# All 16 weight tiles of the second layer's scale modulation as VectorE multiply-adds, landing in two places beside the load ring

## The chip, the cores and the metric

The kernel runs on one core of a Trainium2 chip. The metric is the device time of one execution in microseconds (us); the time before is the median of three runs.

## The reference

Two layers of an adaLN-modulated mixer block over 256 latent and 256 context tokens, D = 2048, all in float32. Cut to what matters here:

```
def modulate(x, norm_g, ada):
    shift, scale, gate = jnp.split(ada, 3, axis=-1)
    return rmsnorm(x, norm_g) * (1 + scale) + shift, gate
...
def mixer_layer(x, xc, c_act, cc_act, norm_g, w_ada, b_ada, w_in, ...):
    h, gate = modulate(x, norm_g, (c_act @ w_ada + b_ada)[:, None, :])
    hc, gate_c = modulate(xc, norm_g, cc_act @ w_ada + b_ada)
    u = h @ w_in
    uc = hc @ (w_in[:, :OFF_MEM_END] if last else w_in)
    ...
    x = x + gate * (jnp.concatenate([y_conv, y_lru, y_attn], axis=-1) @ w_out)
    if not last:
        xc = xc + gate_c * (jnp.concatenate([yc_conv, yc_lru, yc_attn], axis=-1) @ w_out)
```

The change concerns the `scale` third of `c_act @ w_ada + b_ada` and of `cc_act @ w_ada + b_ada` in the second layer: two vectors of 2048, each times a 2048 x 2048 matrix. The weights of layer 1 don't depend on layer 0, so this product can be made while layer 0 is still being computed.

## The kernel before

**Blocks.** Each layer works through 56 blocks of weights of 1 MB (`NB = 56`): blocks 0 to 39 are the input projection (0 to 3 LRU, 4 to 7 keys and values, 8 to 15 convolution, 16 to 31 queries and attention gates, 32 to 39 the other gates), blocks 40 to 55 (`B_OUT = 40`) the output projection, one for each 128 of the output's channels. A block is 16 k-tiles. Float32 products are made of three passes: ScalarE copies a half of the block's weights to a rounded form (`hi`, L1050), VectorE subtracts it from the weights (`lo`, L1410), and TensorE runs high by high, low by high and high by low (L826, L827, L828): 48 matmuls of 512 columns for a block of layer 0.

**The order of work** is written out by hand. Each engine runs its own list, and all of them wait on semaphores. While TensorE is at block b, ScalarE makes `hi` and VectorE `lo` of block b+2, and VectorE brings block b's result out of PSUM (L1596 and L1605 for gate blocks, L1614 for output blocks). SyncE issues the loads in the order of `stream()` into a ring of three slots of 1 MB (`NRAW = 3`, `raw`); a load waits until the tile that had its slot before has been read, and everything behind it in the queue waits too. Behind w(b) for output blocks comes `residual` (L539), which brings 256 KB of the input back for the addition.

**Modulation of layer 1** is made during layer 0 and needs `w_ada` of layer 1, which is 48 tiles of 1 MB (16 each for shift, scale and gate).
- Shift runs on TensorE between blocks: `ada_mm` (L656), four matmuls of 512 columns for a tile, which lie side by side in the array.
- Gate runs on VectorE: `gate_acc(k)` multiplies tile k, one row of the matrix to a partition, by its value of c and adds it to a sum in `kv` (L1441 for tile 0, L1444 for the others). `gate_sum` (L675) adds up over partitions on TensorE at the start of layer 1. In the last two blocks the gate tiles lie ahead of the sums of squares for layer 1's norm (L1467, L1520, L1578 on VectorE, L1091 on ScalarE), which L731 and L733 add up on TensorE.
- Scale is split. Tiles 0 to 7 run on TensorE like shift, two at the end of each of blocks 24, 26, 28 and 30. Tiles 8 to 15 run on VectorE, `scale_acc(k)`: two instructions for a tile, one for c and one for the context's vector, into `qreg` (L1453 for the first tile, L1456 for the others). `scale_sum` (L666, at block `SCALE_SUM = NB - 4`, that is 52) adds the partitions up and onto what TensorE had.

A scale tile of a block up to `SCALE_RING = 39` is loaded into the ring; later ones land in `glu`, which is free by then. `SCALE_ON_DVE` says at which block which tile is added, `gate1_plan()` the same for gate.

**bd** holds the LRU's block-diagonal gate matrices. In layer 0 it also holds keys' parts for attention, until the last group's P·V product (`pv`, L920 to L922, at block 38). GpSimd then clears it for layer 1 (L632), and four small loads (`gate_weights`, L530) bring layer 1's matrices, issued behind the load of block 44. They are first read in layer 1 at 869.7 us (L858).

The functions that the diff touches, and what calls them:

Of the kernel before, what the change touches and what calls it, by code (L numbers as in the profile page):

```python
# [26 lines left out]
DT = D // P  # L27
# [13 lines left out]
SHIFT, SCL, GATE = range(3)  # L41
# [11 lines left out]
NB = len(BLOCKS[0])  # L53
# [31 lines left out]
PW_AT = 35  # L85
LAST_GROUPS = [22, 25, 29, 32]
GATE1_AT = 39
SCALE_ON_DVE = {36: [8], 37: [9], 40: [10], 42: [11], 44: [12], 46: [13], 48: [14], 50: [15]}
SCALE_RING = 39
SCALE_SUM = NB - 4  # L90
TP_LAG = [1, 2]
# [45 lines left out]

def gate1_plan():

    return {B_OUT - 2: [0], B_OUT + 1: [1, 2], **{B_OUT - 1 + k: [k] for k in range(3, DT)}}  # L140

# [108 lines left out]
def program(nc, io, known):  # L252
    ctx = ExitStack()
    with ctx:
# [88 lines left out]
        SLOT, n, ringed = [], 0, 0  # L343
        for i, item in enumerate(STREAM):
            if item[0] == "scale" and item[1] in beside_ring:
                SLOT.append(GLU_SLOT)
            elif i >= opened:
                SLOT.append(ringed % NRAW)
                ringed += 1
            elif item[0] == "chunk":  # L350
                SLOT.append(CHUNK_SLOTS[item[1] % 2])
            else:
                SLOT.append(ADA0_SLOTS[n % len(ADA0_SLOTS)])
                n += 1
# [161 lines left out]
        @block.sync  # L516
        def _(sp):
            sp.dma_start(small[:, 0:N_FIRST], io["small"][:, 0:N_FIRST]).then_inc(*C.up("small_in", by=16))
            for g in range(DT // XPART):
                sp.dma_start(Y[:, XPART * g:XPART * (g + 1), :], io["xT"][:, XPART * g:XPART * (g + 1), :]  # L520
                             ).then_inc(*C.up(f"x_in{g}", by=16))
            sp.dma_start(T[:, 5, 0:3 * P], io["exact"]).then_inc(*C.up("exact_in", by=16))

            def gate_weights(l):

                sp.wait_ge(*(C.at("bd_zero", l) if l not in ROW_GATES else used(last_of(BD_SLOT))))
                for g in range(2):
                    for j in range(2):
                        side, part = (64 * (g ^ j), 0) if l in ROW_GATES else (64 * j, g)
                        sp.dma_start(bd[64 * j:64 * j + 64, part, :, side:side + 64],  # L530
                                     io["lru_w"][l, g, j]).then_inc(*C.up("bd_in", l, g, j, by=16))

            def residual(m):

                if m < 2:
                    sp.wait_ge(*C.at("att_out", 0, max(groups(0))))
                else:
                    sp.wait_ge(*C.at("evac_dve", B_OUT + m - 2))
                sp.dma_start(T[:, m % 2, :], io["xT"][:, m, :]).then_inc(*C.up(f"xs{m % 2}", m, by=16))  # L539

            def turn(l, s):

                b = ROPE_AT[l][s]
                kind, i = BLOCKS[l][b]
                order = list(ROPE_AT[l].values())
                n = order.index(b)
                sp.wait_ge(*C.at("evac_act", l * NB + b))
                if n >= 2:
                    sp.wait_ge(*C.at("rope", l, *BLOCKS[l][order[n - 2]]))
                elif l:  # L550
                    sp.wait_ge(*C.at("ln_n", 0, CT - 1))
                    sp.wait_ge(*C.at("ada_tp", 1, GATE))
                if l == 0:
                    for step, items in PLAN.items():
                        for rows in items:
                            if step < s and rows[2] == DT - 1:
                                sp.wait_ge(*C.at("ada_tp", *rows[:2]))
                for quad in range(0, P, 32):
                    sp.dma_start(turned_of(l, b)[quad:quad + 32, :], rope_of(l, b)[quad ^ 32:(quad ^ 32) + 32, :]
                                 ).then_inc(*C.up(f"turned{n % 2}", l, kind, i, quad, by=16))  # L560

            def turns(item):

                l, s = divmod(item[1] - 1, NB) if item and item[0] == "w" else (0, 0)
                return (l, s) if s in ROPE_AT[l] else None

            for i, item in enumerate(STREAM):
                freed = None
                if SLOT[i] in SLOT[:i]:
                    freed = i - 1 - SLOT[:i][::-1].index(SLOT[i])  # L570
                    sp.wait_ge(*used(freed))
                head = turns(STREAM[freed]) if freed is not None else None
                if head and head[0]:
                    turn(*head)
                dst = slot(i)
                if item[0] == "w":
                    src = io["w_blocks"][item[1]]
                elif item[0] == "chunk":
                    src = io["w_blocks"][0:OPEN[0], :, item[1] * CK * P:(item[1] + 1) * CK * P].rearrange("b p c -> p b c")
                    dst = dst[:, 0:OPEN[0] * CK * P].rearrange("p (b c) -> p b c", b=OPEN[0])  # L580
                elif item[0] == "open":
                    src = io["w_blocks"][NB:NB + SIDE, :, item[1] * QT * P:(item[1] + 1) * QT * P
                                         ].rearrange("b p c -> p b c")
                    dst = dst.rearrange("p (b c) -> p b c", b=SIDE)
                elif item[0] == "ada0":
                    kind, c, g = item[1:]
                    k0, n = group_k(c)
                    rows, cols, at0 = D // n, n * P, kind * D + k0 * P
                    src = io["w_ada"][0, g * rows:(g + 1) * rows, at0:at0 + cols].rearrange("(j p) c -> p j c", p=P)
                    dst = dst.rearrange("p (j c) -> p j c", c=cols)  # L590
                elif item[0] == "pw":
                    src = io["pw"][item[1]]
                elif item[0] == "gate":
                    src = io["w_ada"][1, item[1] * P:(item[1] + 1) * P, GATE * D:(GATE + 1) * D]
                elif item[0] == "scale":
                    if beside_ring and item[1] == beside_ring[0]:
                        sp.wait_ge(*C.at("evac_dve", BLOCKS[0].index(("cg", CT - 1))))
                    src = io["w_ada"][1, item[1] * P:(item[1] + 1) * P, SCL * D:(SCL + 1) * D]
                else:
                    l, kind, k = item[1:]  # L600
                    src = io["w_ada"][l, k * P:(k + 1) * P, kind * D:(kind + 1) * D]
                sp.dma_start(dst, src).then_inc(C.sem(f"raw{SLOT[i]}"), 16)  # L602
                if item == ("chunk", 1):
                    sp.dma_start(small[:, N_FIRST:N_SMALL], io["small"][:, N_FIRST:N_SMALL]
                                 ).then_inc(*C.up("later_in", by=16))
                if item == ("w", OPEN[0] + 1):
                    gate_weights(0)
                if head and not head[0]:
                    turn(*head)
                if item == ("w", B_OUT + 4):  # L610
                    gate_weights(1)
                if item[0] == "w" and 0 <= item[1] - B_OUT - 2 < DT - 2:
                    residual(item[1] - B_OUT - 2)
                elif item[0] == "open" and item[1] < 2:
                    residual(DT - 2 + item[1])
            for m, n in final_parts():
                sp.wait_ge(*C.at("final", m))
                sp.dma_start(io["out"][:, m:m + n, :], Y[:, m:m + n, 0:LAT]).then_inc(*C.up("stored", by=16))
            sp.wait_ge(*C.ago("stored"))
# [3 lines left out]
        def _(pool):  # L623
# [4 lines left out]
            nc.gpsimd.memset(pick[:, 32:33], 1.0).then_inc(*C.up("pick_set"))  # L628
            for l in range(LAYERS):
                if l:  # L630
                    pool.wait_ge(*C.at("pv", l - 1, max(groups(l - 1))))
                    nc.gpsimd.memset(bd[:, :, :, :], 0.0).then_inc(*C.up("bd_zero", l))  # L632
                else:
                    for slot_of_q in Q_SLOTS:
                        pool.wait_ge(*used(last_of(slot_of_q)))
# [9 lines left out]
        def _(pe):  # L645
# [14 lines left out]
            def scale_sum():  # L660

                pe.wait_ge(*C.at("pick_set"))
                pe.wait_ge(*C.at("scale_acc", DT - 1, 1))
                for i in range(2):
                    for j in range(4):
                        last = mm(psA[32 * j:32 * j + 32, :], pick[:, 32 - i:64 - i], scale_part(i)[:, j * TOK:(j + 1) * TOK],  # L666
                                  start=False, stop=(i == 1), tile_position=(0, 32 * j))
                last.then_inc(*C.up("ada_mm", 1, SCL, DT - 1))

            def gate_sum():  # L670
# [1293 lines left out]
```

## Time and profile before

| | |
|---|---|
| median of 3 runs | 1247.78 us (1247.63 to 1248.28) |
| the profiled execution | 1247.64 us |
| its span from first to last instruction | 1245.7 us |
| TensorE clock granted in it, mean | 0.995 of 2.4 GHz |
| busy: TensorE, VectorE, ScalarE | 1203.5, 827.3, 555.5 us |

Some 1.9 us lie outside the span. In rows of the timeline the columns are start (us), duration (us), engine, line, operation, output <- inputs, shape, and in square brackets how long the engine was idle just before and what released it. A row with "x8" stands for eight instructions in a run, with the time of all of them. Matmuls overlap by some 0.15 us at their ends, and other instructions by some 0.08, so that starts, and not durations, are to be compared. Layer 0 ends near 797 us. "+" and "-" in the diff below are lines of the kernel after and before; numbers of lines (L...) are those of the kernel before, unless said otherwise.

### The profile page before, as it was taken

How to read it: one execution, taken by the hardware profiler on the slowest of the kernel's cores; microseconds unless marked ns; L12 is line 12 of the kernel's file. 1: busy time of each engine (PE TensorE's matmuls, PEld its weight loads, DVE VectorE, ACT ScalarE, POOL GpSimd, SP SyncE). 2: the span in 40 equal slices, each digit the busy share in tenths (PEclk: the TensorE clock that was granted, in tenths of full speed). 3: DMA queues.
4: the chain of work that ended last, by engine and by line, in shares of the span. 5: the costliest groups of instructions: out<-in, count | busy, mean ns of one | idle time of the engine just before them, and what ended most of it. 6: DMA issues, size and time to landing. Idle time of an engine off the chain costs nothing.

```text
span 1245.7 us, 16857 instructions
## 1 busy us (share of the span) xinstructions
PE 1203.5 (97%) x6790; PEld 971.9 (78%) x6790; DVE 827.3 (66%) x1268; ACT 555.5 (45%) x873; POOL 10.2 (1%) x13
## 2 busy tenths in 40 slices
PE   2899999999999999999999999999999999999996
PEld 1556777667778777886888887988978988899995
DVE  5444546767666677663787877695899977647554
ACT  5222446652224433464342222354865445475542
POOL 0000100000000000000000001000000000000000
PEclk9999999999999999999999999999999999999998
DMA  9999856556753354211549776343332634325542
GB/s 334 350 349 348 251 208 240 203 207 248 270 218 127 140 187 185 75 68 68 177 158 344 259 286 229 109 145 134 138 106 77 223 133 149 132 102 199 177 170 68
DMA packets 80893, 236.34 MB, mean 190 GB/s; under 512 B 9392, under 2 KB 54192, under 8 KB 59440
## 3 DMA queue, kind: packets, MB, share of 16 engines
q1 hardware_dynamic: 80816, 235.27, 53.5%
q8 instruction: 53, 0.87, 0.3%
q14 instruction: 24, 0.20, 0.1%
HBM read 230.54 MB, written 2.10 MB: 187 GB/s over the span
## 4 chain that ended last, share of the span: by engine, by line
PE 84%; DVE 5%; SPq 4%; DMA 4%; ACT 2%; issue 1%; DVEq 0%; ACTq 0%
PE psum_block L826 21%; PE psum_block L828 21%; PE psum_block L827 21%; SPq L602 3%; PE psum_ada L656 3%; DMA raw<-in_w_ada 2%; PE psum_scores L908 1%; PE psum_scores L895 1%; DVE w_lo L1410 1%; PE psum_scores L928 1%; DVE Y L1691 1%; PE psum_ada L703 1%; DMA glu<-in_w_ada 1%; DMA bd<-in_w_ada 1%; PE psum_misc L955 1%; PE psum_scores L858 1%
## 5 line engine op out<-in xcount | busy, mean ns | idle before, releaser
L826 PE MATMUL psum_block<-h_hi,w_hi 128*128 128x256 f32 (+1 forms) x1648 | 562.4, 341 | 0.6 <-DVE h_lo L1402 0.3
L828 PE MATMUL psum_block<-h_hi,w_lo 128*128 128x256 f32 (+1 forms) x1648 | 553.3, 336 | 0.0
L827 PE MATMUL psum_block<-h_lo,w_hi 128*128 128x256 f32 (+1 forms) x1648 | 553.2, 336 | 0.0
L1410 DVE TENSOR_TENSOR w_lo<-raw,w_hi 128x1024 fp32r<-128x1024 f32 x210 | 254.7, 1223 | 287.7 <-ACT w_hi L1050 287.4
L1050 ACT ACTIVATE w_hi<-raw 128x1024 fp32r<-128x1024 f32 x210 | 220.2, 1057 | 419.5 <-PE psum_block L828 380.0
L826 PEld LDWEIGHTS psum_block<-h_hi,w_hi 128*128 128x128 f32 x1648 | 312.7, 190 | 53.4 <-issue 17.6
L827 PEld LDWEIGHTS psum_block<-h_lo,w_hi 128*128 128x128 f32 x1648 | 312.9, 190 | 33.6 <-issue 2.6
L828 PEld LDWEIGHTS psum_block<-h_hi,w_lo 128*128 128x128 f32 x1648 | 312.7, 190 | 32.4
L1691 DVE SCALAR_TENSOR_TENSOR Y<-glu,small,Y 128x512 f32<-128x512 f32 (+1 forms) x240 | 130.4, 612 | 0.0
L1217 ACT ACTIVATE T<-psum_scores,stats 128x512 f32<-128x512 f32 (+1 forms) x48 | 28.9, 615 | 46.5 <-DVE stats L1739 46.5
L1104 ACT ACTIVATE h_hi<-T,ada 128x256 fp32r<-128x256 f32 x64 | 28.5, 501 | 41.6 <-DVE T L1486 41.6
L1410 DVE TENSOR_TENSOR w_lo<-qreg,w_hi 128x1024 fp32r<-128x1024 f32 (+1 forms) x16 | 17.5, 1092 | 33.4 <-ACT w_hi L1050 32.3
L656 PE MATMUL psum_ada<-raw,cstat 128*32 128x512 f32 x320 | 38.5, 598 | 1.1 <-DVE ada L1475 1.1
L1444 DVE SCALAR_TENSOR_TENSOR kv<-raw,cstat,kv 128x2048 f32<-128x2048 f32 x15 | 35.2, 2344 | 1.1 <-DMA raw<-in_w_ada 1.0
L1223 ACT ACTIVATE T<-T,stats 128x512 f32<-128x512 f32 (+1 forms) x48 | 27.4, 640 | 13.6 <-DVE stats L1749 13.6
L1648 DVE SCALAR_TENSOR_TENSOR Y<-qreg,small,Y 128x512 f32<-128x512 f32 x48 | 32.5, 746 | 0.0
L1050 ACT ACTIVATE w_hi<-qreg 128x1024 fp32r<-128x1024 f32 (+1 forms) x16 | 15.1, 945 | 33.8 <-DMA qreg<-in_w_blocks 33.8
L1079 ACT ACTIVATE T<-Y 128x512 f32<-128x512 f32 (+1 forms) x46 | 24.4, 544 | 10.8 <-DVE Y L1614 8.6
L1492 DVE SCALAR_TENSOR_TENSOR h_lo<-T,ada,h_hi 128x256 fp32r<-128x256 f32 x64 | 27.8, 480 | 1.3 <-ACT h_hi L1104 1.3
L1486 DVE SCALAR_TENSOR_TENSOR T<-Y,A,tbuf 128x256 f32<-128x256 f32 x64 | 27.6, 481 | 0.6
L1456 DVE SCALAR_TENSOR_TENSOR qreg<-glu,cstat,qreg 128x2048 f32<-128x2048 f32 x12 | 27.6, 2345 | 0.0
L1467 DVE TENSOR_TENSOR T<-T 128x512 f32<-128x512 f32 (+1 forms) x42 | 25.1, 598 | 2.8 <-ACT T L1079 1.3
(222 smaller groups left out, 1215.0 us busy)
## 6 DMA issues: line engine op xcount, KB each, us to landing
raw<-in_w_blocks SPq DMA_DIRECT2D x105, 1024.0 KB, 4.8
raw<-in_w_ada SPq DMA_DIRECT2D x75, 1024.0 KB, 7.1
glu<-in_w_ada SPq DMA_DIRECT2D x11, 1024.0 KB, 8.1
qreg<-in_w_blocks SPq DMA_DIRECT2D x8, 896.0 KB, 11.6
kv<-in_w_ada SPq DMA_DIRECT2D x5, 1024.0 KB, 12.0
bd<-in_w_ada SPq DMA_DIRECT2D x5, 1024.0 KB, 11.9
Y<-in_xT SPq DMA_DIRECT2D x8, 512.0 KB, 8.0
T<-in_xT SPq DMA_DIRECT2D x16, 256.0 KB, 5.8
```

The source lines that it names most:

```text
L602: sp.dma_start(dst, src).then_inc(C.sem(f"raw{SLOT[i]}"), 16)
L656: last = mm(psA[32 * j:32 * j + 32, :], cstat[:, c_at(k):c_at(k) + 32], w[:, j * TOK:(j + 1) * TOK], start=(k == 0), stop=(k == DT - 1), t ...
L826: mm(ps[:, cols], hi, hh[:, k, t], start=(at == 0), stop=False)
L827: mm(ps[:, cols], hi, hl[:, k, t], start=False, stop=False)
L828: last = mm(ps[:, cols], lo, hh[:, k, t], start=False, stop=(at == DT - 1))
L1050: fn(wh[:, u % 4, 0:cols.stop - cols.start], raw_of(item)[:, cols], ACT.Copy).then_inc(*C.up("hi", u))
L1104: fn(hh[:, k, tokens(i)], T[:, k % 2, tokens(i)], ACT.Identity, bias=ada[:, l, i, SHIFT * DT + k:SHIFT * DT + k + 1]).then_inc(*C.up("h_hi ...
L1217: fn(T[:, g, k0:TOK], psS[:, g, k0:TOK], ACT.Exp, scale=SCALE, bias=st[:, 1, g:g + 1], accum_out=st[:, 2, g:g + 1]).then_inc(*C.up("att_ex ...
L1410: V.tensor_tensor(wl[:, u % 4, 0:n], raw_of(item)[:, cols], wh[:, u % 4, 0:n].bitcast(F32), ALU.subtract).then_inc(*C.up("lo", u))
L1444: stt(acc, w, cstat[:, c_at(k):c_at(k) + 1], acc, ALU.mult, ALU.add).then_inc(*C.up("gate_acc", k))
L1648: stt(out, x, lcw[:, c, k:k + 1], out, ALU.mult, ALU.add).then_inc(*C.up("taps", l, t, d))
L1691: stt(out, x, dwh[:, c:c + 1], out, ALU.mult, ALU.add).then_inc(*C.up("conv", l, t, k))
```

## The change

All 16 tiles of scale now go through `scale_acc` on VectorE, so that no `ada_mm` of scale is left on TensorE, and `scale_sum` begins the sum in PSUM itself (it therefore waits until shift has been read out of PSUM). Tiles 0 to 4 are added at blocks 36 to 38 and come through the ring. Tiles 5 to 15 are added at blocks 40 to 45 and 47 to 51, one for each block, and land by turns in `glu` and in `bd`. Since `bd` is taken until tile 14 (block 50), it is cleared behind that, and `gate_weights(1)` is issued behind the load of ("open", 0), the first quarter of layer 1's opening blocks. The gate tiles move too: two of them at block 53 and one at 54, and none doubled at block 41.

```
-SCALE_ON_DVE = {36: [8], 37: [9], 40: [10], 42: [11], 44: [12], 46: [13], 48: [14], 50: [15]}
+SCALE_ON_DVE = {36: [0, 1], 37: [2, 3], 38: [4], 40: [5], 41: [6], 42: [7], 43: [8], 44: [9], 45: [10], 47: [11], 48: [12],
+                49: [13], 50: [14], 51: [15]}
...
-    return {B_OUT - 2: [0], B_OUT + 1: [1, 2], **{B_OUT - 1 + k: [k] for k in range(3, DT)}}
+    return {B_OUT - 2: [0], B_OUT + 1: [1], **{B_OUT + k: [k] for k in range(2, DT - 3)}, NB - 3: [13, 14], NB - 2: [15]}
...
             if item[0] == "scale" and item[1] in beside_ring:
-                SLOT.append(GLU_SLOT)
+                SLOT.append((GLU_SLOT, BD_SLOT)[beside_ring.index(item[1]) % 2])
...
-                    if beside_ring and item[1] == beside_ring[0]:
+                    if item[1] == beside_ring[0]:
                         sp.wait_ge(*C.at("evac_dve", BLOCKS[0].index(("cg", CT - 1))))
+                    elif item[1] == beside_ring[1]:
+                        sp.wait_ge(*C.at("pv", 0, max(groups(0))))
...
-                if item == ("w", B_OUT + 4):
+                if item == ("open", 0):
                     gate_weights(1)
...
-                    pool.wait_ge(*C.at("pv", l - 1, max(groups(l - 1))))
+                    pool.wait_ge(*C.at("scale_acc", beside_ring[-1 - len(beside_ring) % 2], 1))
...
                 pe.wait_ge(*C.at("scale_acc", DT - 1, 1))
+                pe.wait_ge(*C.at("ada_out", 1, SHIFT))
...
-                                  start=False, stop=(i == 1), tile_position=(0, 32 * j))
+                                  start=(i == 0), stop=(i == 1), tile_position=(0, 32 * j))
```

VectorE's list at blocks 36 and 37, before; L1453 and L1456 are scale tiles (two instructions each), L1410 is `lo` of a block's half, L1729 the low part of the attention weights, which TensorE's P·V product waits for.

```order
L1453 TENSOR_SCALAR qreg<-raw,cstat 128x2048 x2
L1410 TENSOR_TENSOR w_lo<-raw,w_hi 128x1024 x2
L1596 SCALAR_TENSOR_TENSOR tbuf<-tbuf,psum_block 128x512
L1605 SCALAR_TENSOR_TENSOR Y<-tbuf,glu 128x512
L1729 TENSOR_TENSOR T_r<-psum_scores,T_r 128x2x128 x4
L1456 SCALAR_TENSOR_TENSOR qreg<-raw,cstat,qreg 128x2048 x2
L1410 TENSOR_TENSOR w_lo<-raw,w_hi 128x1024
```

The same place of VectorE's list after the change, where these lines are numbered four higher.

```order
L1457 TENSOR_SCALAR qreg<-raw,cstat 128x2048 x2
L1460 SCALAR_TENSOR_TENSOR qreg<-raw,cstat,qreg 128x2048 x2
L1414 TENSOR_TENSOR w_lo<-raw,w_hi 128x1024 x2
L1600 SCALAR_TENSOR_TENSOR tbuf<-tbuf,psum_block 128x512
L1609 SCALAR_TENSOR_TENSOR Y<-tbuf,glu 128x512
L1733 TENSOR_TENSOR T_r<-psum_scores,T_r 128x2x128 x4
L1460 SCALAR_TENSOR_TENSOR qreg<-raw,cstat,qreg 128x2048 x4
L1414 TENSOR_TENSOR w_lo<-raw,w_hi 128x1024
```

A second tile now stands behind the first at block 36, ahead of the two `lo` of block 39, and another behind block 37's, ahead of block 40's `lo`. Two rows further on, at block 38, a tile stands for the first time behind gate tile 0 (L1441), ahead of block 41's `lo` and of the twelve L1402 that split the output projection's left side for TensorE.

SyncE's queue at the end of layer 0, before; `in_w_ada` are the gate tiles 13, 14 and 15, `128x2048` of `in_w_blocks` the load of block 55, the two of `128x4x512` are ("open", 0) and ("open", 1), and L539 is `residual`.

```order
L602 DMA raw<-in_w_ada 128x2048
L602 DMA raw<-in_w_blocks 128x2048
L539 DMA T<-in_xT 128x512
L602 DMA raw<-in_w_ada 128x2048
L602 DMA raw<-in_w_blocks 128x4x512
L539 DMA T<-in_xT 128x512
L602 DMA raw<-in_w_ada 128x2048
L602 DMA raw<-in_w_blocks 128x4x512
```

The same place of SyncE's queue after the change, from block 55's load on.

```order
L605 DMA raw<-in_w_blocks 128x2048
L540 DMA T<-in_xT 128x512
L605 DMA raw<-in_w_ada 128x2048 x2
L605 DMA raw<-in_w_blocks 128x4x512
L531 DMA bd<-in_lru_w 64x8x64 x4
L540 DMA T<-in_xT 128x512
L605 DMA raw<-in_w_ada 128x2048
L605 DMA raw<-in_w_blocks 128x4x512
```

Gate tiles 13 and 14 now stand together ahead of ("open", 0), and four small loads stand between ("open", 0) and gate tile 15. The ring slot that ("open", 0) takes was gate tile 13's before, which is added at block 52; now it is block 55's, so that the load waits for `lo` of block 55. Gate tile 15's slot was block 55's and is now gate tile 13's, which is added at block 53.

## Rows read from the trace of the kernel before

**Rows 1.** The page: busy time of each engine, and the costliest group of instructions.
```profile
PE 1203.5 (97%) x6790; PEld 971.9 (78%) x6790; DVE 827.3 (66%) x1268; ACT 555.5 (45%) x873; POOL 10.2 (1%) x13
...
L826 PE MATMUL psum_block<-h_hi,w_hi 128*128 128x256 f32 (+1 forms) x1648 | 562.4, 341 | 0.6 <-DVE h_lo L1402 0.3
```

**Rows 2.** Timeline of TensorE at block 24, around two scale tiles.
```profile
433.29 0.28 PE L883 MATMUL psum_scores<-bd_r,T_r 128*128 128x256 f32 x1
433.50 1.92 PE L656 MATMUL psum_ada<-raw,cstat 128*32 128x512 f32 x16
...
435.69 0.39 PE L827 MATMUL psum_block<-h_lo,w_hi 128*128 128x512 f32 x1
```

**Rows 3.** Timeline of TensorE where the same products stand without scale tiles.
```profile
591.38 0.28 PE L883 MATMUL psum_scores<-bd_r,T_r 128*128 128x256 f32 x1
...
591.73 0.39 PE L827 MATMUL psum_block<-h_lo,w_hi 128*128 128x512 f32 x1
```

**Rows 4.** Timeline of VectorE, 597 to 637 us: each row with idle time, and both ends.
```profile
597.70 2.45 DVE L1453 TENSOR_SCALAR qreg<-raw,cstat 128x2048 f32<-128x2048 f32 x2
600.52 1.22 DVE L1410 TENSOR_TENSOR w_lo<-raw,w_hi 128x1024 fp32r<-128x1024 f32 x1 [0.36 <-ACT w_hi L1050]
603.74 1.23 DVE L1410 TENSOR_TENSOR w_lo<-raw,w_hi 128x1024 fp32r<-128x1024 f32 x1 [1.99 <-ACT w_hi L1050]
...
616.89 1.23 DVE L1410 TENSOR_TENSOR w_lo<-raw,w_hi 128x1024 fp32r<-128x1024 f32 x1 [3.02 <-ACT w_hi L1050]
...
622.33 1.23 DVE L1410 TENSOR_TENSOR w_lo<-raw,w_hi 128x1024 fp32r<-128x1024 f32 x1 [1.69 <-ACT w_hi L1050]
...
627.28 4.91 DVE L1402 TENSOR_TENSOR h_lo<-Y,h_hi 128x512 fp32r<-128x512 f32 x8 [1.32 <-ACT h_hi L1269]
...
636.38 0.69 DVE L1402 TENSOR_TENSOR h_lo<-Y,h_hi 128x512 fp32r<-128x512 f32 x1
```

**Rows 5.** Timeline of TensorE, the wait inside block 40.
```profile
637.12 0.50 PE L826 MATMUL psum_block<-h_hi,w_hi 128*128 128x512 f32 x1 [0.34 <-DVE h_lo L1402]
```

**Rows 6.** Timeline of VectorE and TensorE, 693 to 769 us.
```profile
693.68 1.23 DVE L1410 TENSOR_TENSOR w_lo<-raw,w_hi 128x1024 fp32r<-128x1024 f32 x1 [0.35 <-ACT w_hi L1050]
...
760.10 0.87 DVE L1614 SCALAR_TENSOR_TENSOR Y<-psum_block,ada,T 128x256 f32<-128x256 f32 x2
...
768.58 0.64 PE L666 MATMUL psum_ada<-qreg,pick 128*32 128x512 f32 x4
```

**Rows 7.** Windows: stretch, length, busy of PE PEld DVE ACT POOL, clock, DMA share, GB/s.
```profile
35.00:40.00 5.00, 3.46 (x14) 1.79 (x15) 3.26 (x7) 2.40 (x5) 0.00 (x0) 0.66 1.10 349
656.00:659.00 3.00, 3.00 (x14) 2.46 (x14) 2.08 (x2) 1.06 (x1) 0.00 (x0) 1.00 1.29 249
660.00:780.00 120.00, 120.00 (x540) 97.92 (x539) 89.70 (x80) 29.59 (x34) 3.81 (x2) 1.00 0.74 276
```

**Rows 8.** Timeline of SyncE's queue at block 42, and gate tile 15's issue.
```profile
651.41 0.33 SPq L602 DMA_DIRECT2D raw<-in_w_blocks  x1
...
656.45 0.42 SPq L602 DMA_DIRECT2D raw<-in_w_ada  x1
...
784.59 0.33 SPq L602 DMA_DIRECT2D raw<-in_w_ada  x1
```

**Rows 9.** Landing time of the load issued at 656.45 us, by its line.
```profile
DMA to landing us min/median/max: 5.8/5.8/5.8
```

**Rows 10.** Timeline of VectorE, ScalarE and TensorE at the end of layer 0.
```profile
789.56 2.35 DVE L1444 SCALAR_TENSOR_TENSOR kv<-raw,cstat,kv 128x2048 f32<-128x2048 f32 x1 [0.95 <-DMA raw<-in_w_ada]
791.83 0.68 DVE L1467 TENSOR_TENSOR T<-T 128x512 f32<-128x512 f32 x1
...
793.70 0.48 DVE L1578 SCALAR_TENSOR_TENSOR Y<-psum_block,ada,T 128x256 f32<-128x256 f32 x1 [0.66 <-PE psum_block L828]
...
794.22 0.42 ACT L1091 ACTIVATE T<-Y 128x256 f32<-128x256 f32 x1 [5.16 <-DVE Y L1578]
...
796.81 0.59 PE L733 MATMUL psum_scores<-T,small 128*128 128x256 f32 x2
```

## The prediction

> **What bounds the kernel now.** I read the page first. TensorE is busy for 1203.5 us, 97% of the span, and VectorE for 827.3; the 1648 matmuls that begin each k-tile waited for 0.6 us in all, 0.3 of it at one place for L1402 [rows 1]. So an instruction that leaves TensorE is worth its time as long as nothing else becomes late at that place, and one added to VectorE costs nothing as long as it fits into idle time there. Both hold by stages only, so I went through the timelines of the stages that the change touches: blocks 24 to 31, which lose the tiles; blocks 36 to 40, where VectorE gets three more of them; blocks 41 to 51, one tile each; and the end of layer 0, where loads change places. My sum is made against the profiled execution's own 1247.64 us; the median of the runs shown, 1247.78, lies 0.14 above it. A measurement of this kernel can tell about 0.2%, or 2.5 us, from no change.
>
> **Blocks 24 to 31: what goes.** From L883 at 433.29 to the block's L827 at 435.69 are 2.40 us with two scale tiles between them [rows 2]; from the same L883 to the same L827 are 0.35 without (591.38 to 591.73) [rows 3]. Two tiles cost 2.05 us, and four groups of them -8.2; the other three groups read 2.00 to 2.07 in the same manner, so I take **-8.1**. Could another wait fill the gap? TensorE's matmuls of blocks wait almost nowhere now [rows 1], and each group hands the next block over only 2 us sooner, with eight loads fewer in flight; so I take nothing back, with bounds -8.0 and -8.3 from the readings of the four groups.
>
> **Blocks 36 to 40: three more tiles.** VectorE's list there gets a second tile at block 36, a second at 37 and one at 38, each two multiply-adds. The step from the start of such an instruction of 2.35 us to the next is 2.27 (789.56 to 791.83) [rows 10]; six cost 13.6. Between the first scale tile at 597.70 and the last part of the output projection's left side, L1402 at 636.38, VectorE idles 0.36 + 1.99 + 3.02 + 1.69 + 1.32 = 8.4 us [rows 4]. It waits there for ScalarE's copies, which wait for TensorE, and for the left side's high part; when VectorE is behind, those are done before it comes to them. Where an idle time vanishes, the 0.08 us by which instructions overlap is gained as well, some 0.4 for five. So VectorE is late by 13.6 - 8.4 - 0.4 = 4.8 at 636.38, and from 597.70 it has no gap left. That row is one that TensorE already waits for: 0.34 us until 637.12 [rows 5]. All of it therefore stands on the path: **+4.7** at the end of block 40, less what ends of matmuls take up. It won't show as one wait. By my own recurrence of the lists, P·V at block 38 waits some 0.6 to 0.9 for L1729, the start of block 40 some 3 us for the first of the L1402, and two more places in block 40 the rest. Bounds: 4.4, if 0.3 of the present wait takes some up; 6.0, if loads become late. These tiles come through the ring of three slots, and the tile of block 38 can only be loaded when the second tile of block 36 is read; by the recurrence it lands half a microsecond before it is wanted, at a landing time of 4.9, and a landing of 5.8 [rows 9] would put 0.4 to 1.2 more on the path.
>
> **Blocks 41 to 51: one tile a block.** A block takes TensorE 10.88 us (48 products at 0.227). Before, a block with a scale tile left VectorE a wait of 0.35 before the second `lo` [rows 6], and 0.57 or so elsewhere; so one in every block fits, barely, and VectorE's lag of block 40 is gone by block 42. Nothing is added to the path. At the end, the sum over partitions waits for tile 15: the block's result comes out at 760.10 in block 51, behind it stand a gate tile, L1467 and the two scale instructions (2.26 + 0.6 + 4.6, and 0.8 for the result itself), which ends at 768.4; L666 is at 768.58 [rows 6]. Slack 0.2, cost 0 to 0.2. GpSimd's clearing of bd has 20 us from tile 14 to the matrices' loads, and the matrices are read first in layer 1 at 869.7: hidden, and 80 us of cover would have to go before it costs anything.
>
> **The end of layer 0: gate tile 15 comes later.** Before, it was issued at 784.59 [rows 8], as soon as `lo` of block 55 was done, and VectorE took it up at 789.56 after a wait of 0.95 for it [rows 10]. Now ("open", 0) is issued at that moment, and behind it come four small loads, a residual and only then tile 15. The same sequence stands in the trace of before, at block 42: a load of 1 MB at 651.41, the four small ones, a residual, and the next load at 656.45, which is 5.04 us of SyncE [rows 8]; that next load landed 5.8 later [rows 9]. So tile 15 lands near 784.59 + 5.04 + 5.8 = 795.4. Queued behind it on VectorE are its multiply-add (2.27), L1467 (0.6, and 0.2 to the next), L1520 (0.34), L1578 (0.5), then ScalarE's square L1091 (0.42), which L733 waits for: 799.7 to 799.8. L733 stood at 796.81 [rows 10], so **+2.9**. The second gate tile of block 53 costs 2.27 of VectorE, but it lies ahead of the landing and vanishes in that wait. Bounds: 0, if tile 15 lands by 791 (VectorE would come to it 1.3 later than now, and between L1091 at 794.22 and L733 lie 2 us); 3.9, if it lands a microsecond later still. I take the row's value, since the same requests stand in the same order.
>
> Here a rule speaks against the row. While those small loads moved, the rate was 249 GB/s with the DMA engines over 100% busy (656 to 659), and 349 in a stretch of large loads (35 to 40) [rows 7]. The Trainium skill (page "DMA: Bandwidth & Descriptors", sections "Specifications" and "Why small descriptors are slow") has it that transfers under 512 bytes miss the line rate, and that a 256-byte descriptor pays about 27% more on the bus. The matrices' pieces are 256 bytes; by that figure alone half a megabyte at 349 GB/s would take 1.5 us, with the surcharge 1.9 (an estimate from that page), tile 15 would land near 792, and the transition would cost almost nothing. The trace agrees that they are slow, but the 5.04 us of the queue are more than the page's figure gives.
>
> **Sum.** -8.1 + 4.7 + 0 + 2.9 = -0.5; 1247.64 - 0.5 = 1247.1. I say **1247.2**, with 0.1 for the slack of L666. By the page's figure on small descriptors the sum would be some 1244.3.
>
> **Rivals.**
> - *Faster: tile 15 isn't held back* (22%). If SyncE passes the small loads on quickly, or they don't slow the one behind, it lands by 791 to 792 and the +2.9 shrinks to 0 or 0.3: 1244.2. Against it speak the 5.04 us of rows 8; for it, that at block 42 other large loads were in flight, and at 784 there are few.
> - *The clock falls in a new gap* (12%). After a gap and amid short bursts near 35 us, the granted clock was 0.66 over 5 us [rows 7], that is two thirds of the time at 1.2 instead of 2.4 GHz; 3.46 us of TensorE work at 0.66 are some 1.2 us lost, by my reading up to 1.7. New gaps of 3 us are to come in block 40 and at L731. In block 40 a slow clock is taken up in part by TensorE's further waits (0.4 left); at the end of layer 0 the full 1.7 counts. +0.4 to +2.1, and with it 1249. The Trainium skill (page "TensorE: Matmul & The Clock Gate", section "What's actually happening") says that an idle TensorE is throttled to 1.2 GHz and activity releases it; rows 7 agree that both levels occur, not that a gap of 3 us is enough.
> - *Slower: the loads of blocks 41 to 51 don't keep up* (14%). A block now brings its own 1 MB, a gate tile, a scale tile and 256 KB: 3.41 MB in 10.88 us, or 313 GB/s, for ten blocks; before it was that in every second block, 276 on the mean of 660 to 780 with the engines 74% busy [rows 7]. It decides at a sustained rate of 313. At 300 a block takes 11.4 us, and ten blocks +5: 1252. Against it: 349 is seen over 5 us at 35, and 0.74 x 313/276 is 84% of the engines' time. For it: VectorE has no block left in which to catch up but block 46, so that each late landing stays.
> - The change does what it says; what it removes is plain in the list of TensorE.
>
> **How the numbers follow.** The forecast holds with 52%, with 1246 to 1249 as its own range. Between -8.3 + 4.4 + 0 = -3.9 and -8.0 + 6.0 + 3.9 + 2.1 = +4.0 the known terms give 1243.7 to 1251.6. To hold 8 in 10, I take in the faster rival and the clock, and leave out the slow loads and the worst of the bounds: 1244.0 to 1250.6. Faster by over 0.2% (below 1245.3): the faster rival and a little of the forecast's edge, 24%. Slower (above 1250.3): the slow loads and a little of the clock's, 16%. Within: 60%.
>
> **What would show it.** Right: no L656 between L883 and L826 at blocks 24 to 30, and block 32 8.1 us earlier; VectorE without a gap from its first scale tile to block 40; a wait of about 3 us of TensorE at the start of block 40 on L1402, and of 0.6 to 0.9 on L1729 at block 38; blocks 41 to 51 at 10.88 us each; VectorE waiting for the DMA of the last gate tile for 4 to 5 us, and TensorE for about 3 at L731 and L733. Wrong would make it: waits for DMA at scale tiles in blocks 41 to 51; L731 not waiting; a clock under 1 behind block 40; a scale tile of blocks 36 to 38 that lands after VectorE asks for it.

## The result and the profile after

The changed kernel takes 1250.01 us (median of 20 runs, 1248.03 to 1250.93), the kernel before 1247.88 (20 runs, 1247.33 to 1248.77). The ratio is 1.0015 with a 95% interval of 1.0009 to 1.0021: 0.15% or 2.1 us slower, which is within the 0.2% of the forecast's "no change", and on the other side of zero from its -0.6. The profiled execution, at 1248.03, is the lowest of the 20 and so shows less than a typical one loses; three more profiled executions of the same kernel follow below.

The page of the profile after, its first lines of engines and of costly groups, which answer to [rows 1]; L830 is L826 of before.

```profile
PE 1198.5 (96%) x6726; PEld 971.6 (78%) x6726; DVE 862.6 (69%) x1284; ACT 556.5 (45%) x873; POOL 10.2 (1%) x13
...
L830 PE MATMUL psum_block<-h_hi,w_hi 128*128 128x256 f32 (+1 forms) x1648 | 562.8, 341 | 4.0 <-DVE h_lo L1406 2.8
```

TensorE lost 64 matmuls and VectorE gained 16 instructions and 35 us. The matmuls of that line now wait 4.0 us where they waited 0.6, and of that 2.8 is for the split of the output projection's left side, in block 40.

The timeline of VectorE and TensorE after the change at blocks 36 to 40, to be read against [rows 4, 5].

```profile
589.10 2.45 DVE L1457 TENSOR_SCALAR qreg<-raw,cstat 128x2048 f32<-128x2048 f32 x2
591.46 4.61 DVE L1460 SCALAR_TENSOR_TENSOR qreg<-raw,cstat,qreg 128x2048 f32<-128x2048 f32 x2
...
600.91 9.13 DVE L1460 SCALAR_TENSOR_TENSOR qreg<-raw,cstat,qreg 128x2048 f32<-128x2048 f32 x4
...
632.50 0.69 DVE L1406 TENSOR_TENSOR h_lo<-Y,h_hi 128x512 fp32r<-128x512 f32 x1
...
601.05 0.50 PE L924 MATMUL psum_scores<-T_r,bd_r 128*128 128x512 f32 x1 [0.78 <-DVE T_r L1733]
...
621.84 0.77 PE L830 MATMUL psum_block<-h_hi,w_hi 128*128 128x512 f32 x1 [2.79 <-DVE h_lo L1406]
```

From the first scale tile to the last part of the left side are 43.40 us (589.10 to 632.50); before they were 38.68 (597.70 to 636.38). VectorE is 4.7 us late there. None of its rows in that stretch has idle time in brackets any more. TensorE shows that lateness at two places: 0.78 for the attention weights' low part, 2.79 at the start of block 40. The rest went into a fall of the clock at the same place, as the first row of this view of windows shows (stretch, length, busy of PE PEld DVE ACT POOL, clock, DMA share, GB/s).

```profile
620.00:630.00 10.00, 8.16 (x30) 6.71 (x31) 9.96 (x16) 8.37 (x16) 0.00 (x0) 0.83 0.05 17
795.00:805.00 10.00, 8.46 (x65) 8.01 (x66) 7.46 (x13) 6.25 (x10) 0.00 (x0) 1.00 0.00 2
```

In the kernel before, the clock held at both places:

```profile
630.00:635.00 5.00, 5.00 (x23) 4.14 (x23) 4.97 (x9) 5.00 (x9) 0.00 (x0) 1.00 0.16 25
795.00:800.00 5.00, 5.00 (x41) 4.89 (x41) 1.71 (x2) 2.81 (x3) 0.00 (x0) 1.00 0.01 3
```

Behind the gap of 2.79 us the granted clock is 0.83 on the mean of ten us, which is a third of the time at 1.2 GHz and the rest at 2.4. Slower matmuls then reach the later parts of the left side after VectorE has made them, so that a second wait is missing (the one execution in which the clock held there has it, see after_again).

The end of layer 0 after the change: SyncE's queue, VectorE and TensorE, to be read against [rows 8, 10].

```profile
780.83 0.38 SPq L605 DMA_DIRECT2D raw<-in_w_blocks  x1
781.25 2.69 SPq L531 DMA_DIRECT2D bd<-in_lru_w  x4
783.99 1.74 SPq L540 DMA_DIRECT2D T<-in_xT  x1
785.77 0.44 SPq L605 DMA_DIRECT2D raw<-in_w_ada  x1
...
790.43 0.48 DVE L1582 SCALAR_TENSOR_TENSOR Y<-psum_block,ada,T 128x256 f32<-128x256 f32 x1 [3.52 <-DMA T<-in_xT]
792.85 2.35 DVE L1448 SCALAR_TENSOR_TENSOR kv<-raw,cstat,kv 128x2048 f32<-128x2048 f32 x1 [1.94 <-DMA raw<-in_w_ada]
...
791.06 0.36 PE L830 MATMUL psum_block<-h_hi,w_hi 128*128 128x256 f32 x1 [1.17 <-DVE Y L1582]
...
796.39 0.70 PE L735 MATMUL psum_scores<-T,small 128*128 128x256 f32 x2 [2.22 <-DVE T L1524]
797.24 0.70 PE L737 MATMUL psum_scores<-T,small 128*128 128x256 f32 x2
...
806.49 1.06 PE L679 MATMUL psum_ada<-kv,small 128*32 128x512 f32 x8
```

The first opening quarter goes out at 780.83, and gate tile 15 at 785.77, 4.94 us of SyncE later. Its landing is here, in the view of that one load:

```profile
DMA to landing us min/median/max: 7.1/7.1/7.1
```

VectorE waits for two loads in a row, the residual (3.52) and tile 15 (1.94), and TensorE then for VectorE (1.17 and 2.22).

A table by stage, worked out from rows like these. Its columns are the start of VectorE's first scale tile; from there to the sum over partitions (`scale_sum`); from there to the second sum of squares (L733 before, L737 after); from there to `gate_sum` (L675, L679); and from there to the end of the span. It holds all profiled executions; each is a single one, while the times given with the experiments are medians of several.

| execution | first scale tile | to scale_sum | to L733 | to gate_sum | to the end | its time |
|---|---|---|---|---|---|---|
| before | 597.70 | 170.88 | 28.23 | 9.15 | 439.7 | 1247.64 |
| after | 589.10 | 175.72 | 32.42 | 9.25 | 439.4 | 1248.03 |
| after_again | 589.68 | 175.62 | 32.45 | 10.77 | 439.4 | 1250.02 |
| after_third | 589.78 | 176.01 | 32.62 | 10.55 | 439.3 | 1250.46 |
| after_fourth | 589.69 | 175.84 | 32.58 | 9.25 | 439.3 | 1248.84 |
| matrices_late | 589.35 | 175.95 | 29.98 | 9.26 | 439.3 | 1245.99 |
| gates_spread | 589.85 | 176.02 | 28.23 | 9.14 | 439.4 | 1244.74 |
| two_on_pe | 592.10 | 170.86 | 32.49 | 10.79 | 439.3 | 1247.67 |
| spread15 | 590.46 | 170.91 | 28.23 | 9.14 | 439.4 | 1239.94 |
| spread16 | 589.78 | 174.02 | 28.24 | 9.14 | 439.3 | 1242.64 |

### The profile page after: what moved, and what is told of

The parts are those of the page before. It is cut to its first block, busy times and chain, and to the rows that moved or that the text cites. A ratio compares the mean times of both kernels' runs of the same rounds, so it can differ in the third digit from the quotient of the medians.

```text
span 1245.9 us, 16752 instructions
## 1 busy us (share of the span) xinstructions
PE 1198.5 (96%) x6726; PEld 971.6 (78%) x6726; DVE 862.6 (69%) x1284; ACT 556.5 (45%) x873; POOL 10.2 (1%) x13
## 4 chain that ended last, share of the span: by engine, by line
PE 82%; DVE 5%; SPq 4%; DMA 4%; ACT 2%; issue 1%; DVEq 0%; ACTq 0%
PE psum_block L830 21%; PE psum_block L831 21%; PE psum_block L832 21%; SPq L605 3%; PE psum_ada L659 2%; DMA raw<-in_w_ada 2%; DVE w_lo L1414 1%; DVE qreg L1460 1%; PE psum_scores L899 1%; PE psum_scores L862 1%; PE psum_scores L912 1%; DMA glu<-in_w_ada 1%; PE psum_ada L707 1%; DMA bd<-in_w_ada 1%; PE psum_misc L959 1%
## 5 line engine op out<-in xcount | busy, mean ns | idle before, releaser
L830 PE MATMUL psum_block<-h_hi,w_hi 128*128 128x256 f32 (+1 forms) x1648 | 562.8, 341 | 4.0 <-DVE h_lo L1406 2.8
L830 PEld LDWEIGHTS psum_block<-h_hi,w_hi 128*128 128x128 f32 x1648 | 313.2, 190 | 53.8 <-issue 17.3
L659 PE MATMUL psum_ada<-raw,cstat 128*32 128x512 f32 x256 | 30.8, 598 | 1.2 <-DVE ada L1479 1.2
```

Source lines behind the costliest of these rows:

```text
L659: last = mm(psA[32 * j:32 * j + 32, :], cstat[:, c_at(k):c_at(k) + 32], w[:, j * TOK:(j + 1) * TOK], start=(k == 0), stop=(k == DT - 1), t ...
L830: mm(ps[:, cols], hi, hh[:, k, t], start=(at == 0), stop=False)
```

## The experiments

**Three more profiled executions of the changed kernel: after_again, after_third, after_fourth.** No edit. What was expected of the first:

> The changed kernel once more, one look. Its first profiled execution took 1248.03 us, the lowest of its 20 times, whose median is 1250.01, so something that differs between executions by 2 us is missing from that trace. Theory A (the clock): the new gaps of TensorE, 2.8 us at the start of block 40 and some 3.4 at L735, sometimes let the granted clock fall and sometimes not; this execution shows a window of the end of layer 0 (790 to 800 us) or of blocks 40 and 41 with a granted clock below the 1.00 and 0.66 of the first one, and is longer by 1 to 3 us. Theory B (landing): gate tile 15 or the residual lands later than the 7.1 and 9.4 us after issue that the first one shows, with the same clock. Either would be seen by the time between L735 and the end of block 40.

of the second:

> The changed kernel, a third look. Theory A (a fall of the clock behind the wait at L735 is what typical executions have and the first one, 1248.03, did not): this execution is near 1250 if the granted clock falls below 1.00 between 795 and 805 us, and near 1248 if it does not; the two times differ by 1.7 to 2 us, and the time from L737 to L679 is 9.25 without a fall and 10.8 with one, as in the first two looks. Theory B (landings differ): the waits for the residual and for tile 15 differ from 3.5 and 1.9 to 2.0 us by more than 0.5.

and of the third:

> The changed kernel, a fourth look, with the same expectations as the third: 1250 with a fall of the clock between 795 and 805 us, 1248 without; theory B would show other waits at the residual or tile 15.

The executions took 1250.02, 1250.46 and 1248.84 us. These are the windows of after_again at block 40 and at the end of layer 0, and TensorE's second wait in block 40.

```profile
620.00:630.00 10.00, 7.57 (x33) 6.30 (x34) 9.96 (x16) 8.76 (x17) 0.00 (x0) 1.00 0.13 50
795.00:805.00 10.00, 7.94 (x48) 7.42 (x49) 6.67 (x10) 5.19 (x8) 0.00 (x0) 0.83 0.01 3
...
633.83 0.50 PE L830 MATMUL psum_block<-h_hi,w_hi 128*128 128x512 f32 x1 [0.58 <-DVE h_lo L1406]
```

Here the clock held in block 40 and fell behind the wait at L735. The way from L737 to `gate_sum` took 10.77 us instead of 9.25, and in after_third, where the clock is 0.83 in the same stretch, 10.55; in after_fourth and in the first execution, with 1.00, 9.25. The waits for the residual (3.50 to 3.67) and for tile 15 (1.94 to 2.00) are the same in all four, so theory B falls. Most of what is left between the four, up to 0.7 us, is when the first scale tile starts. The fall in block 40 costs little: 175.62 without it, in the one execution that lacks it, and 175.72 to 176.01 with it. There TensorE has a second wait to give up, which in after_again shows as 0.58 us.

**matrices_late.** The four small loads go behind the third opening quarter.

```
-                if item == ("open", 0):
+                if item == ("open", 2):
                     gate_weights(1)
```

> The four small loads of the gate matrices stand behind the third opening quarter's load, not the first's; all else as changed. Theory A (small loads hold back gate tile 15 and the residual ahead of it): tile 15 is issued as soon as gate tile 13 has been added, near 784, and lands near 789; VectorE's waits for the residual (3.5 us) and for tile 15 (1.9) vanish or shrink to 1.5 together, TensorE's 2.2 and 1.2 us at L735 and L830 go to 0.7 or less in all, and the time is 1246 to 1247 (3 us below the changed kernel's 1250.0, 1 below the kernel before). If the gap also cost a fall of the clock in typical executions, 1245. Rival (what delays tile 15 is that the first opening quarter now waits for block 55's low part): the waits stay above 2 us and the time is 1249.5.

1246.45 us (11 runs), ratio to before 0.9989 (0.9980 to 0.9998): 3.6 us below the changed kernel. The wait for the residual is gone. That for tile 15 isn't:

```profile
781.99 4.80 DVE L1448 SCALAR_TENSOR_TENSOR kv<-raw,cstat,kv 128x2048 f32<-128x2048 f32 x2
...
784.36 0.33 SPq L605 DMA_DIRECT2D raw<-in_w_ada  x1
...
790.90 2.35 DVE L1448 SCALAR_TENSOR_TENSOR kv<-raw,cstat,kv 128x2048 f32<-128x2048 f32 x1 [3.12 <-DMA raw<-in_w_ada]
...
794.44 0.70 PE L735 MATMUL psum_scores<-T,small 128*128 128x256 f32 x2 [1.18 <-DVE T L1524]
```

Tile 15 now waits for its slot, which is gate tile 13's: that one is added from 781.99, and the issue follows at 784.36; with the quarter's megabyte, issued 3 us ahead, still under way, it lands 6.5 us later. The stage keeps 1.75 us of its 4.2 (29.98 against 28.23). So the small loads cost 2.4 us there, and the doubled gate tile of block 53 with the new slots the rest. The time came out as theory A had it, but the wait of 3.1 us for tile 15 as its rival did: each had a part. The clock stayed at 1.00 behind the shorter wait, in this one execution.

**gates_spread.** The doubled gate tile stands at block 46, where no scale tile is, so that no tile is doubled at 53; the small loads stay where the change put them.

```
-    return {B_OUT - 2: [0], B_OUT + 1: [1], **{B_OUT + k: [k] for k in range(2, DT - 3)}, NB - 3: [13, 14], NB - 2: [15]}
+    return {B_OUT - 2: [0], B_OUT + 1: [1], **{B_OUT + k: [k] for k in range(2, 6)}, B_OUT + 6: [6, 7],
+            **{B_OUT - 1 + k: [k] for k in range(8, DT)}}
```

> Gate tiles 6 and 7 both at block 46, where no scale tile stands, and from there one tile a block up to 15 at block 54; the small loads stay behind the first opening quarter. That quarter then takes the slot of gate tile 13, added at block 52, as before the change, and is issued some 10 us earlier, the small loads with it. Theory A (small loads hold back what is behind them): they are through before tile 15 is issued near 781, tile 15 lands 4.9 us later, the transition costs nothing: 1246, some 4 us below the changed kernel. VectorE at block 46 has 4.6 us of work less than the blocks around it, so two gate tiles cost nothing. Rival (blocks 41 to 51 are too full for another shift of loads): TensorE waits at blocks 46 to 48, and the time stays at 1249 to 1250.

1244.63 us (7 runs, 1243.68 to 1244.94), ratio 0.9971 (0.9961 to 0.9982), 5.4 below the changed kernel.

```profile
771.42 0.38 SPq L606 DMA_DIRECT2D raw<-in_w_blocks  x1
771.85 2.75 SPq L532 DMA_DIRECT2D bd<-in_lru_w  x4
...
781.88 0.33 SPq L606 DMA_DIRECT2D raw<-in_w_ada  x1
...
786.70 2.35 DVE L1449 SCALAR_TENSOR_TENSOR kv<-raw,cstat,kv 128x2048 f32<-128x2048 f32 x1 [0.81 <-DMA raw<-in_w_ada]
```

The first opening quarter has gate tile 13's slot again and goes out at 771.42, ten us earlier; the same four small loads cost 2.75 us of SyncE (2.69 in the changed kernel), but tile 15 isn't behind them. It lands in 4.8 us, VectorE waits 0.81 for it, and the stage is 28.23 us, as before the change. So it isn't the small loads alone, but the small loads ahead of a load that is due. The time is 1.4 us below what was expected; the stage accounts for 4.2 of the 5.4, and the rest is about what the clock's fall at the end of layer 0 costs in the executions that have it.

**two_on_pe.** Two tiles back on TensorE, so that blocks 36 to 38 have two tiles instead of five; gates and small loads as changed.

```
+SCALE_ON_DVE = {36: [2], 37: [3], **{B_OUT + k: [4 + k] for k in range(12)}}
...
-                                  start=(i == 0), stop=(i == 1), tile_position=(0, 32 * j))
+                                  start=False, stop=(i == 1), tile_position=(0, 32 * j))
```

> Scale tiles 0 and 1 back on TensorE at block 24, 2 and 3 alone at blocks 36 and 37, and the other twelve at blocks 40 to 51, one each; gates and small loads as changed. So blocks 36 to 38 have one tile each at 36 and 37, as before the change. Theory A (the backlog of VectorE at blocks 36 to 40 costs 4.8 us): TensorE's waits at P.V (0.8) and at the start of block 40 (2.8) vanish, the clock of 620 to 625 is 1.00 and not 0.66, block 24 gets its 2.05 us back, and the time is 2.7 us below the changed kernel's, 1247.3; with the fall of the clock in block 40 counted in full, 1246. Rival (the loads through the ring, not VectorE, are what is late at block 40): with two ring loads fewer there the waits would go too, but VectorE would show waits for DMA there in the changed kernel, which it doesn't. Second rival: twelve scale tiles in twelve blocks, without the pause at block 46, let VectorE fall behind: +1 to +2, scale_sum waiting.

1247.14 us (11 runs), ratio 0.9993 (0.9985 to 1.0002), 2.9 below the changed kernel. TensorE waits in block 40 as it did before the change, and nowhere else there:

```profile
631.50 0.50 PE L829 MATMUL psum_block<-h_hi,w_hi 128*128 128x512 f32 x1 [0.34 <-DVE h_lo L1405]
...
795.00:800.00 5.00, 4.86 (x25) 4.38 (x24) 2.98 (x2) 3.10 (x4) 0.00 (x0) 0.66 0.00 0
```

The stage to `scale_sum` is 170.86 us, as before (170.88): the backlog costs 4.8 to 5.1 us, and scale tiles in all of blocks 40 to 51, without the pause at 46, cost nothing. The end of layer 0 still has its 4.3 us and, in this execution, the fall of the clock (10.79, second row).

**spread15 and spread16.** Both parts put together: one gate tile a block, from 1 at block 40 to 15 at 54, and a scale tile in each of blocks 40 to 51. spread15 adds one tile at 36, two at 37, none at 38, and leaves tile 0 to TensorE (its `ada_plan` takes a group of one tile, and `scale_sum` adds onto it as in two_on_pe); spread16 adds tile 0 on VectorE too.

```
 spread15
+SCALE_ON_DVE = {36: [1], 37: [2, 3], **{B_OUT + k: [4 + k] for k in range(12)}}
 spread16
+SCALE_ON_DVE = {36: [0], 37: [1, 2], 38: [3], **{B_OUT + k: [4 + k] for k in range(12)}}
 both
+    return {B_OUT - 2: [0], **{B_OUT - 1 + k: [k] for k in range(1, DT)}}
```

> Fifteen scale tiles on VectorE: one at block 36, two at 37 behind the attention weights' low part, none at 38, one each at blocks 40 to 51; tile 0 alone on TensorE. One gate tile a block: 0 at 38, 1 at 40, up to 15 at 54, none doubled; small loads behind the first opening quarter, which is then issued as early as before the change. Theory A: blocks 24 to 31 give back seven tiles, 7.1 us; VectorE's 8.4 us of idle time at blocks 36 to 40 hold the one more tile (4.5 us) without a new wait on the path; the end of layer 0 costs nothing: 1240.8, faster than the kernel before by 7 us and than the changed one by 9. Rival (any tile more at blocks 36 to 40 is on the path, since TensorE already waits there): +4.5, 1245.3, with waits at P.V or at the start of block 40. Second rival: gate and scale in each of blocks 40 to 51 are too much for the loads or VectorE: scale_sum waits, 1243 or more.

> As the run with fifteen, and tile 0 on VectorE as well: one tile at block 36, two at 37, one at 38, one each at 40 to 51. Theory A (VectorE's idle time of 8.4 us holds one more tile and most of a second, 9.0, and of that only what stands ahead of each L1402 counts): the tile at block 38 has 3.0 us of idle time behind it and puts 1.5 to 1.9 us on the path at block 40, against 1.0 that TensorE gets back: 1241.3 to 1241.8, 0.5 to 0.9 above the run with fifteen. Rival (the tile fits): 1239.8, TensorE's wait at block 40 below 0.5.

spread15: 1239.94 us (5 runs, 1239.76 to 1240.91), ratio 0.9937 (0.9925 to 0.9950): 0.6% faster than the kernel before, and faster than the changed one. That is 0.9 below what was expected; 0.3 to 0.4 of it lies behind `gate_sum`, where every changed version is that much shorter than the kernel before, and why isn't shown. Its VectorE and TensorE at blocks 36 to 40:

```profile
600.29 9.13 DVE L1459 SCALAR_TENSOR_TENSOR qreg<-raw,cstat,qreg 128x2048 f32<-128x2048 f32 x4
...
615.17 1.23 DVE L1413 TENSOR_TENSOR w_lo<-raw,w_hi 128x1024 fp32r<-128x1024 f32 x1 [0.35 <-ACT w_hi L1053]
...
620.03 4.91 DVE L1405 TENSOR_TENSOR h_lo<-Y,h_hi 128x512 fp32r<-128x512 f32 x8 [1.23 <-ACT h_hi L1272]
...
629.86 0.50 PE L829 MATMUL psum_block<-h_hi,w_hi 128*128 128x512 f32 x1 [0.33 <-DVE h_lo L1405]
```

The second tile of block 37 used up the 3.02 us and most of the 1.69 of [rows 4], and TensorE's wait is what it was. spread16: 1242.34 us (5 runs), ratio 0.9953 (0.9940 to 0.9967), 2.4 above spread15, more than the 0.5 to 0.9 that I expected. I had given its tile at block 38 the idle time of the kernel before; in spread15 only 0.35 + 1.23 = 1.6 us of it are left there, so that 4.5 - 1.6 = 2.9 us come onto the path, against 1.0 that TensorE gets back. In the profiled execution TensorE shows 1.88 of it as a wait at the start of block 40, with the clock at 0.83 from 620 to 630, and the stage is 3.1 us longer than in spread15.

```profile
620.53 0.47 PE L829 MATMUL psum_block<-h_hi,w_hi 128*128 128x512 f32 x1 [1.88 <-DVE h_lo L1405]
```

## Why the prediction was wrong

The sum gave -0.5 and the runs +2.1. Two of its steps failed: gate tile 15's landing at the end of layer 0 was mis-sized by 1.3 us, and a fall of the clock behind the new gap there, 1.3 to 1.5 us in the executions that have it, was put at nothing. Added to the sum, the two give +2.1 to +2.3.

**What left TensorE: right.** -8.1 was forecast; the first scale tile starts 7.9 to 8.6 us earlier in the four executions of the changed kernel.

**Blocks 36 to 40: right.** +4.7 was forecast; the stage grew by 4.7 to 5.1, and two_on_pe takes all of it back. The waits came where they were placed (0.78 for a forecast 0.6 to 0.9, 2.79 for 3). "A clock under 1 behind block 40" was named as a sign of being wrong; it came in three of the four executions and cost little.

**Blocks 41 to 51: right.** No wait of TensorE stands there in any run. The rival of loads that don't keep up is out.

**The end of layer 0: the mechanism right, the size not.** This is the term that was mis-sized: +2.9 was forecast, the stage grew by 4.2 to 4.4 in the four executions. SyncE's 5.04 us were 4.94, but tile 15 landed 7.1 us after its issue where I had taken 5.8 from block 42; that is 1.3 us. Why it took longer than the same requests at block 42 no run shows. I had also held the doubled gate tile of block 53 to be free because it vanishes in the wait for the landing. It isn't when the small loads are gone: matrices_late keeps 1.75 us, since tile 15's new slot is gate tile 13's. And the residual, which I counted as a request of the queue only, landed 3.5 us after VectorE wanted it; in the changed kernel that lies under tile 15, and so the wait for tile 15 itself was 1.9 and not the forecast 4 to 5.

**The clock: a term left out of the sum.** The rival "the clock falls in a new gap" was given 12% and +0.4 to +2.1. It came true at the end of layer 0 in two of the four executions, each with 1.3 to 1.5 us, within the 1.2 to 1.7 that the prediction had for it. The typical time agrees with it: -8.0 + 4.8 + 4.2 is 1.0, and with the fall 2.4, against 2.1 between the medians. That step was wrong as the prediction put it: the fall belonged in the sum, not among the rivals. The versions without the gap (before, gates_spread, spread15, spread16) show the clock at 1.00 there. The spread of times says less: the changed kernel's 20 lie within 2.9 us, gates_spread's 7 within 1.3, but the kernel before has 1.4 in one set of 20 and 2.2 in another of 23. That the gap brings the fall on is what these traces agree on and is not shown by itself, as I have not filled the gap with other work; why one execution has the fall and the next not stays open. In block 40 a fall cost 0.1 to 0.4 us against the one execution without it, at most the 0.4 that was forecast.

The Trainium skill's figure on small descriptors (page "DMA: Bandwidth & Descriptors", section "Why small descriptors are slow"), as the prediction used it, would have put the end of layer 0 near zero. The measurement decides against it as a price here: half a megabyte of 256-byte pieces took 2.69 us of SyncE's queue, the residual behind it another 1.74, and the next megabyte 7.1 until it had landed.

## What to carry to other kernels

Moving work to an engine with idle time pays as far as that idle time lies ahead of the engine's next deadline: add it up row by row up to the row that the bottleneck waits for, and place the added work behind that row's producers. spread15 gets 8 us from the same idea, with one tile fewer on VectorE and one gate tile to a block. When a load is moved, follow the requests behind it on its queue to the first one that is due, and let the ring's slots tell which load waits for which. A new gap of 2 to 3 us on TensorE should be counted with a fall of its clock behind it, 1.3 to 1.5 us here in about half of the executions, unless a later wait takes that up.

## What the runs showed of the hardware

- A gap of TensorE of 2.8 us in block 40 was followed by a granted clock of 0.83 over ten us in five of six executions (three of the changed kernel's four, matrices_late and gates_spread). Gaps of 1.1 to 1.3 and 2.2 to 2.3 us at the end of layer 0, with some 3 us of matmuls between them, were followed by a fall in three of five (two of the changed kernel's four, and two_on_pe). The same program on the same data had it or not.
- Such a fall cost 1.3 to 1.5 us where TensorE sets the pace behind it, and 0.1 to 0.4 where TensorE had to wait again for VectorE.
- Behind four loads of 128 KB in 256-byte pieces, a request of 256 KB held SyncE for 1.74 us in the changed kernel and 1.65 in the kernel before, instead of 0.50. The next megabyte landed 7.1 us after its issue in the changed kernel and 5.8 in the kernel before, instead of 4.8 (gates_spread) and 4.9 (before) where nothing else was under way.
